# A two-block transformer kernel in split fp32: the opening's orders in the filter and the mixer changed, and the forgetting attention with tiles halved around its logits, named PSUM banks and values products behind the tiles

## The reference

```python
def hybrid_mixer(h, w_in, b_forget, conv_w, conv_b, conv_ln_g, conv_ln_b, w_out):
    z = h @ w_in                      # a 512, g 512, q 512, k 512, v 512, f 8 columns
    ...
    u = a * jax.nn.sigmoid(g)
    u = causal_depthwise_conv(u, conv_w, conv_b)             # width 31
    u = jax.nn.silu(layer_norm(u, conv_ln_g, conv_ln_b))
    log_f = jax.nn.log_sigmoid((f_logit + b_forget).astype(jnp.float32))
    att = forgetting_attention(q.reshape(shp), k.reshape(shp), v.reshape(shp), log_f)
    ...
    return jnp.concatenate([u, att], axis=-1) @ w_out

def forgetting_attention(q, k, v, log_f):      # 8 heads of 64, blocks of 128 rows, causal
    ...
        logits = logits + cum[:, :, q0:kl, None] - cum[:, :, None, :kl]
        p = jax.nn.softmax(jnp.where(mask, logits, NEG_INF), axis=-1)

x = x + rms_norm(hybrid_mixer(rms_norm(x, g), ...), g2)
x = x + rms_norm(memory_cross_attention(rms_norm(x, g), rms_norm(mem, g), ...), g2)
x = x + rms_norm(squared_relu_mlp(rms_norm(x, g), w_up, w_down), g2)
# second block: MLA layer and Hyena layer (FFT convolutions with learned filters), each with a conv FFN
```

## Time and profile before

| | us |
|---|---|
| runs | 2100.52, 2098.52, 2098.56, median 2098.56 |
| profiled execution | 2100.5 |
| its span | 2098.7 |
| PE busy | 2011.9 (96%) |
| PE weight load busy | 1672.6 (80%) |
| DVE busy | 1272.0 (61%) |
| POOL busy | 983.0 (47%) |
| ACT busy | 861.7 (41%) |

### The profile page before, as it was taken

The page is one execution under the profiler, slowest core; times in us unless marked ns, Lnnn a source line. Parts: engine busy times, 40 slices in busy tenths (PEclk is TensorE's granted clock), DMA queues, the critical chain, the costliest instruction groups (busy, mean ns, idle before and its releaser), DMA issues.

```text
span 2098.7 us, 23678 instructions
## 1 busy us (share of the span) xinstructions
PE 2011.9 (96%) x9667; PEld 1672.6 (80%) x9667; DVE 1272.0 (61%) x1568; ACT 861.7 (41%) x1254; POOL 983.0 (47%) x476
## 2 busy tenths in 40 slices
PE   6999989999999999999999999999998999999997
PEld 4777778778888887787888888878887888888886
DVE  7677845462245435663677775545679657778644
ACT  5746775631122234774443333232322244333322
POOL 5579454454444433123444444444667654444443
PEclk9999999999999999999999999999999999999999
DMA  6432123112222230121222222215222312222221
GB/s 206 154 123 81 41 81 106 65 71 101 101 99 86 97 113 27 43 71 47 71 86 98 101 101 100 84 63 185 101 71 101 121 61 101 100 101 92 89 101 40
DMA packets 35041, 193.00 MB, mean 92 GB/s; under 512 B 4400, under 2 KB 4992, under 8 KB 15413
## 3 DMA queue, kind: packets, MB, share of 16 engines
q1 hardware_dynamic: 34932, 191.49, 26.1%
HBM read 177.77 MB, written 13.64 MB: 91 GB/s over the span
## 4 chain that ended last, share of the span: by engine, by line
PE 77%; DVE 11%; ACT 6%; POOL 4%; issue 2%; DMA 0%; SPq 0%; ACTq 0%; DVEq 0%; POOLq 0%
PE ps L159 73%; PE ps L158 3%; DVE TMP L182 2%; POOL WL L182 1%; POOL CO L182 1%; DVE X L182 1%; DVE X L194 1%; DVE YL L182 1%; PE ps L167 1%; DVE ps L194 1%; POOL YF L182 1%; DVE ps L182 1%; ACT WH L175 1%; ACT PP L176 0%; DVE VG L182 0%
## 5 line engine op out<-in xcount | busy, mean ns | idle before, releaser
L182 POOL TENSOR_TENSOR WL<-W,WH 128x2048 fp32r<-128x2048 f32 (+3 forms) x165 | 650.5, 3948 | 860.5 <-ACT WH L175 857.0
L159 PE MATMUL ps<-HH,WL 128*128 128x512 f32 (+1 forms) x1408 | 545.6, 388 | 15.4 <-DVE HL L194 7.9
L159 PE MATMUL ps<-HH,WH 128*128 128x512 f32 (+1 forms) x1408 | 538.8, 383 | 0.0
L159 PE MATMUL ps<-HL,WH 128*128 128x512 f32 (+1 forms) x1408 | 538.8, 383 | 0.0
L175 ACT ACTIVATE WH<-W 128x2048 fp32r<-128x2048 f32 (+2 forms) x145 | 269.4, 1858 | 316.8 <-PE ps L159 316.8
L159 PEld LDWEIGHTS ps<-HH,WL 128*128 128x128 f32 x1408 | 265.3, 188 | 74.9 <-DVE HL L194 9.9
L159 PEld LDWEIGHTS ps<-HH,WH 128*128 128x128 f32 x1408 | 265.2, 188 | 51.9
L159 PEld LDWEIGHTS ps<-HL,WH 128*128 128x128 f32 x1408 | 265.6, 189 | 50.7 <-issue 0.2
L182 DVE TENSOR_TENSOR MRL<-MID,MRH 128x512 fp32r<-128x512 f32 x76 | 177.4, 2365 | 162.3 <-ACT MRH L175 162.3
L159 PE MATMUL ps<-MRH,WL 128*128 128x512 f32 x608 | 238.2, 392 | 3.3 <-ACT PAD L175 2.2
L159 PE MATMUL ps<-MRH,WH 128*128 128x512 f32 x608 | 236.7, 389 | 0.0
(11 more groups left out here) (370 smaller groups left out, 3284.3 us busy)
## 6 DMA issues: line engine op xcount, KB each, us to landing
W<-in_up SPq DMA_DIRECT2D x44, 1024.0 KB, 4.8
W<-in_down SPq DMA_DIRECT2D x22, 1024.0 KB, 4.8
W<-in_w_up SPq DMA_DIRECT2D x16, 1024.0 KB, 4.8
W<-in_w_down SPq DMA_DIRECT2D x16, 1024.0 KB, 4.8
W<-in_hy_in SPq DMA_DIRECT2D x12, 1024.0 KB, 4.8
kd<-STG SPq DMA_DIRECT2D x36, 256.0 KB, 2.0
KB<-kd SPq DMA_DIRECT2D x8, 1024.0 KB, 5.8
W<-in_win_ag SPq DMA_DIRECT2D x4, 1024.0 KB, 4.8
```

The source lines that it names most:

```text
L159: return self.eng.matmul(out, lhs, rhs, start=start, stop=stop)
L182: return QUIET if self.eng is None else self.eng.tensor_tensor(out, a, b, op)
```

## The change

The chunks of q and k: the first one (tiles 0 and 1) is put ahead of v's two, so chunk 6 is qk, 7 and 8 are v, 9 to 11 the others. In the filter PE waits for the first half of chunk 0's low part alone, copies of WP are done earlier on ACT and POOL, and ACT's copies of x for the first norm (`x_high`) are parted from the squares (`x_square`). In the mixer's start, the column sums and transposes of the norm and the forget gate are done between the tiles of "ag". Tiles of q and k from 3 on are cut into two halves, one before the logits of the next head and one behind; banks are named (`on(i)` sets the turn), three (`here`) for this head's transposes and values, and three (`there`) for the next head's logits. The convolution's steps on DVE are 6 at head 0 and 14 at head 1 in place of 7 a head; the memory norm's scaling and the centring of the convolution come at heads 3 and 4; the squares of the centred values are made by POOL; the first chunk of w_out takes its k tiles in the order 4, 5, 6, 0, 1, 2, 3, 7. The DMA of the constants `tri` is issued ahead of chunk 6.

```diff
 
 CHUNKS = [
-    ("dft_cs", 0, 2048), ("dft_kx", 0, 256), *[("win_ag", i, 2048) for i in range(4)], *[("win_v", i, 2048) for i in range(2)],
-    *[("win_qk", i, 2048) for i in range(4)], *[("w_mk", i, 2048) for i in range(2)],
+    ("dft_cs", 0, 2048), ("dft_kx", 0, 256), *[("win_ag", i, 2048) for i in range(4)], ("win_qk", 0, 2048),
+    *[("win_v", i, 2048) for i in range(2)], *[("win_qk", i, 2048) for i in range(1, 4)], *[("w_mk", i, 2048) for i in range(2)],
...
-
-                wh, wl = chunk(n)
+                if (n, part) == (0, 0):
+                    pe.wait_ge(*at("w_high", n))
+                    pe.wait_ge(*at("w_low", n, "first"))
+                    wh, wl = place(n)
+                else:
...
 
             def turn_f(n):
 
                 if n == 0:
+                    column_sum([(("xcol",), DG, ("xacc", 7), None, ("xcol",))])
+                if n == 2:
+                    spread("rs", 0, slot=4)
+                if n == 4:
                     ps = open_bank("ft_")
                     pe.wait_ge(*at("fs_"))
                     for b in range(4):
                         ins = pe.turn(ps[:, 8 * b:8 * b + 8], FZ[:, blk(b)], IDT[0:8, 0:8])
...
+                turn[0] = i
+
+            def qk_steps(n, first, last):
+                wh, wl = chunk(CH["win_qk"][n // 2])
+                ps = bank("qk", n) if first else open_bank("qk", n)
+                for k in range(first, last + 1):
+                    col = (2 * k + n % 2) * 128
+                    ins = pe.mm3(ps[:], wh[:, col:col + 128], wl[:, col:col + 128], *feat(k), k == 0, k == 7)
+                if last == 7:
+                    ins.then_inc(*up(acc, ("qk", n), *[("w_used", CH["win_qk"][n // 2])] * (n % 2)))
+
+            qk_steps(0, 0, 7)
+            qk_steps(1, 0, 7)
             vb = [open_bank("v", b) for b in range(4)]
...
-                for i in range(4):
+
+                def mask(i):
+                    if i != 1:
+                        on(places[max(i - 1, 0)])
+                        open_bank("fs", h, max(i, 1))
                     nk = 128 * (i + 1)
                     pe.mm(logits(h, i)[:, nk - 128:nk], IDR[:], MKR[:], i != 1, False, True)
+
+                for i in range(3):
+                    mask(i)
...
                 for i in range(4):
+                    if i == 3:
+                        mask(3)
                     nk = 128 * (i + 1)
...
+                for k in (4, 5, 6, 0, 1, 2, 3, 7):
+                    pe.wait_ge(*at("cat", k))
...
+            fox_s(0, (g0, g1, v1))
+            on(v2)
+            qk_steps(2, 0, 7)
+            here, there = [g0, g1, v1], [v0, v2, v3]
             for h in range(8):
-                fox_t(h)
+                fox_t(h, here)
+                if h < 5:
+                    on(there[2])
+                    qk_steps(h + 3, 0, 3)
+                if h == 5:
+                    mem_k(0, (0, 1), 0, 3, (c0, c1))
                 if h < 7:
-                    fox_s(h + 1)
+                    fox_s(h + 1, (there[0], there[1], here[0]))
+                if h < 5:
+                    qk_steps(h + 3, 4, 7)
+                if h == 5:
+                    mem_k(0, (0, 1), 4, 7)
+                if h == 6:
+                    on(there[2])
+                    column_sum([(("cq2",), CO2[:, j, :], ("csq", j), None, ("cq2",) if j == 3 else None)
+                                for j in range(4)])
+                    mem_k(1, (0,), 0, 7, (here[2],))
                 if h == 7:
-                    mem_k(1, 1)
-                qk_tile(h + 4)
-                fox_pv(h)
+                    mem_k(1, (1,), 0, 7, (c0,))
+                    on(c1)
+                    spread("crs", slot=20)
...
                     spread("mr", slot=28, nb=2)
-                if h == 4:
-                    total("cmu", ap=DG[:], need=("cacc", 3))
...
-                if h == 5:
-                    mem_k(0, 0, 1)
-                if h == 6:
...
+                    on(c0)
+                    total("cmu", ap=DG[:], need=("cacc", 3))
+                here, there = [there[0], there[1], here[0]], [there[2], here[1], here[2]]
...
-                act.wait_ge(*at("h", 1, 1, 3, 1))
+                act.wait_ge(*at("wpt", 1, 1, 1))
                 act.act(HH[:, k, :], X[:, k, :], ACT.Identity, par("g_mix_pre", k)).then_inc(*out(("hn", 0, k, "hi")))
+
...
+                        if m == 3 and o == 0 and c == 0:
                             wp_high(0, 1, 0)
                             wp_high(0, 1, 1)
+                        if m % 2 and o == 1:
+                            x_high(4 * c + m - 1)
+                            x_high(4 * c + m)
                 for c in range(2):
...
+            qk_high(0)
+            products(9, 12)
+            qk_high(1)
+            weights(8)
+            products(13, 16)
+            weights(9)
+            for b in range(4):
+                act.wait_ge(*at("v", b))
...
                     dst = QKB[e, j % 2][0:64, 1, :] if m else QKA[e, j % 2][64 - 64 * e:128 - 64 * e, 0, :]
                     low(dst, bank("qk", n)[hd, :], QKA[e, j % 2][hd, m, :], ("k" if m else "q", j, e),
                         *[("free", "qk", n)] * e)
-                if n < 2:
-                    convolve(4, 3)
+
+            convolve(2, 3)
+            qk_out(0)
+            convolve(6, 3)
+            qk_out(1)
+            convolve(20, 3)
...
                     low(PTL[:, q], bank("ft", h, j)[:, 0:q.stop - q.start], PTH[:, q], ("pt", h, j), ("free", "ft", h, j))
+                if h == 6:
+                    mem_k_low(0, 1)
                 if h < 7:
                     fox_max(h + 1)
-                    convolve(3, 3)
-                    if h in (4, 5):
-                        scaled_memory(4 * h - 16, 4 * h - 15)
+                    if h == 1:
+                        convolve(3, 3)
+                    if h in (3, 4):
+                        scaled_memory(4 * h - 12, 4 * h - 9)
                     fox_rcp(h + 1)
-                    if h in (4, 5):
-                        scaled_memory(4 * h - 14, 4 * h - 13)
-                convolve(4, 3)
+                if h == 0:
+                    convolve(6, 3)
+                if h == 1:
+                    convolve(200, 3)
+                if h in (3, 4):
+                    centred(2 * h - 6, 2 * h - 5)
                 if h == 7:
-                    for j in range(4):
-                        low(HL[:, j, :], CO[:, j, :], HH[:, j, :], ("cat", j))
-                qk_out(h + 4)
-                fox_low(h)
...
-            h_low(4, 7)
+            h_low(4, 5)
             wp_low(0, 1, 0)
...
+            taps(11, 16)
             weights(9)
-            taps(15, 24)
+            taps(17, 19)
             weights(10)
+            taps(20, 24)
             twins(2)
...
-            weights(6)
             sp.wait_ge(*at("rs", 0))
             load("tri", DG[:], t["consts"][:, 256:768])
+            weights(6)
```

233 lines of the change are left out of this document (121 added, 112 removed).

## The result

The change takes 2107.15 us (median of 5 runs, 2104.97 to 2109.34) against 2100.11 us (2098.52 to 2100.76) for the kernel before: a ratio of 1.0039 with a 95% interval of 1.0027 to 1.005. It is slower by 0.39%; 2096 in a range of 2084 to 2107 was predicted, and a gain was the likelier sign.

What follows compares the result with a forecast made beforehand. PE, busy 96% of the span, bounds the kernel, so only waits and low clock can be won. PE's count and clock gave -5.9, chunk 15 took back 1.9, one fall 1.6: -2.2, so 2096 us, range 2084 to 2107.

Steps and rivals of the forecast that it cites:

- 1.2 for the first w_out chunk: Heads 3 to w_out: 1.2 us of PE wait at that chunk, within 3.0 us of small waits.
- -2.2: Predicted shift at the second w_out chunk, counting one clock fall of 1.6 us, before the third head's logits.
- t(0): First transposes: a wait of 2.2 us in place of 3.32, ending at 197.0, 2.6 us ahead in PE's count.
- MRS: Tile 4's first half waits for ACT to free its bank, behind six convolution steps: about +3.3 us.
- fox_s(3): Head 3's logits wait for tile 4's bank, freed by DVE behind eleven convolution steps: about +4.6, taken as 5.0 us.
- three falls, +1.0: Case where each of three new waits costs a 1.6 us clock fall, making the shift +1.0 us.
- The filter's term: Opening: the 1.85 us WP wait and the low clock after it go, about -3.6 us.
- now stand inside it: Start: column sums and spreads (1.6 us) move from ahead of the gate GEMM into it; net so far -4.0 us.
- A: Rival, chance 0.26: waits at heads 0 to 2 are shorter; 2090.6 us, down to 2084.
- C: Rival, chance 0.12: the filter edit does nothing, so 3.6 us of gain is gone; 2100 us, up to 2103.
- B: Rival, chance 0.20: DVE, ACT and PE loop at heads 0 to 2, head 3's logits wait 8 us; 2104, up to 2108.
- D: Rival within the forecast's 0.42: POOL's additions slowed beside DVE's convolutions, chunk 8 ready 2.6 us later; 2099 us.

Runs made afterwards that it cites:

- free banks: The change with the first w_out tiles opened in two other banks that are free early, nothing else; 2100.69 us, ratio 1.001.
- early copy: As free banks, and ACT copies the second w_out chunk ahead of the four silu steps; 2100.93 us, ratio 1.001.
- the filter alone: The kernel before with only the filter's part of the change; 2093.15 us, ratio 0.9978.
- filter and start: The kernel before with the change's filter part, mixer start and earlier constants DMA, v and heads as before; 2097.37 us, ratio 0.999.
- convolution behind tiles: As free banks, with DVE's convolution steps of heads 0 and 1 placed behind qk_out and fox_low; 2100.68 us, ratio 1.0006.
- chunk 8 early: As early copy, with ACT's copy of v's second half ahead of products 9 to 12 and POOL's low part behind tap 8; 2097.76 us.
- convolution spread: As chunk 8 early, with DVE's convolution steps spread over heads 0 to 2 and all centring at head 4; 2096.81 us, ratio 0.9987.
- the filter undone: The change with its filter edits taken out, all else kept, w_out banks too; 2108.69 us, ratio 1.006.

## Why the prediction was wrong

**The step that failed** is "1.2 for the first w_out chunk" among the small waits. It measured 6.07, and 6 us at clock 0.53 followed, 2.8 us more. I had followed the data of that chunk (the cat tiles, its low part) and took the banks for free; the tenant of `there[1]` is head 7's values. With other banks alone 5.44 us of the +7.55 go, which is shown; 1.93 us for chunk 15 come in that wait's place. Without that the change is +2.1 at the landmark and 2100.69 us.

**The rest, from -2.2 to +2.1, stands ahead of w_out, and most of it is clock.** With the free banks PE is ready for chunk 15 at 306.1 us (308.06 less the wait of 1.93), where the sum has 301.7 (300.1 and one fall). The wait itself came out as forecast, 1.93 for 1.9; chunk 15 is late by as much as PE, behind silu, CATH and a table load in ACT's queue, and the early copy shows that this place is worth 1.1 us. The 4.4 us are: 2.6 at the end of t(0) (199.6 in place of 197.0), which come from the gates (below); 1.7 for a fall behind MRS, at 213, that I had not counted; 0.9 since the low clock behind fox_s(3) took 2.5 and not 1.6; less 1.3 of waits that were shorter. About 0.5 stays open. Of the forecast's cases the one with three falls, +1.0, was the nearest, though t(0) had none.

**What held.** WP's wait went, its copies now at 41.14. Gates at 97.24 (97.2 predicted), with a wait of 1.99. Chunk 5 took the constants' wait back: 1.52 (2.0 predicted). Chunk 8: 3.65 (3.7), though PE and the chunk both came 2.4 us later than in the sum. MRS: 3.34 (3.3). fox_s(3), 4.21 (4.6 to 5.0), by the low parts of QKA behind the eleven steps. Heads 3 to 7: 0.7 + 1.27 (1.8). t(0): 0.73 (2.2), the one that was well off; PE came there later.

**The filter and the start.** The filter's term held: at its last matmuls PE is 3.8 us ahead in the change and 3.9 with the filter alone, where I had 3.6. What was wrong in the opening is my reading of the start, "now stand inside it" at no loss. At 120 us the change is 1.5 us ahead where I had 4.0. Of these 2.5 us, 1.7 is the fall behind the wait at 97.24 (it did not come in three of the seven profiles with this wait), and the rest is time of PE for the sums.

**Rivals.** A (short waits at heads 1 and 2) and C (no filter gain) did not happen. B has the right sign, but its mechanism, the loop of DVE, ACT and PE, did not: fox_s(3) waited 4.2 us and not 8. D: chunk 8's low part was ready at 175.8 us, 2.3 later than the 173.5 of the sum, but D is not the reason: POOL's squares started at 151.41 and not at 149.2, with the gates late, and six of its additions took 8.16 us, 1.36 each as before.

## What to carry to other kernels

A reordering is bounded by the banks as much as by the data: when the order of k is changed so that the late tile comes last, list the last tenant of every bank that the first matmul opens. Work that is moved away may have stood in the shade of a copy or a low part; ask first what PE would do there instead. Look at the instruction that frees or copies for the next chunk, and how deep it stands in ACT's and DVE's queues: the w_out banks were worth 5.4 us here, the place of chunk 8's copy about 3. And before a shift between two profiles is put down to an edit, compare the granted clock behind each wait that both have: here the same wait fell in one and not in the other, at 1.6 to 3 us a time, as much as several of the edits.

## What the runs showed of the hardware

The length of a wait alone did not decide on the clock. A wait of 1.99 us at 127.75 in the kernel before was followed by full clock (1.00 in the earlier trace rows, and in the next window below); the wait of 1.99 us for WL in the change by 0.68. That wait, at the same place behind the same instructions, stands in seven profiles: the clock fell in four (the change, free banks, early copy, filter and start) and held in three (convolution behind tiles, chunk 8 early, convolution spread).

The same holds where the whole program is the same. In the kernel before, that next window, and in the second block two waits and the windows around them:

```profile
129.90:152.10 22.20, 22.20 (x98) 17.93 (x97) 17.95 (x26) 11.81 (x13) 19.29 (x13) 1.00 0.16 52
...
1596.78 0.63 PE L167 MATMUL ps<-IDT,TMP 128*128 128x128 f32 x4 [2.32 <-DVE ZL L182]
...
1648.53 0.79 PE L159 MATMUL ps<-HYH,WL 128*128 128x512 f32 x1 [2.00 <-POOL HYL L182]
...
1596.00:1602.00 6.00, 5.22 (x21) 4.26 (x21) 4.16 (x9) 0.60 (x1) 4.71 (x6) 0.72 0.84 339
1648.00:1653.00 5.00, 4.47 (x13) 3.58 (x14) 4.86 (x9) 1.41 (x5) 5.00 (x7) 0.66 1.01 419
```

The same two waits in the changed kernel, and the windows 7.5 us later:

```profile
1604.42 0.63 PE L167 MATMUL ps<-IDT,TMP 128*128 128x128 f32 x4 [2.31 <-DVE ZL L182]
...
1654.59 0.50 PE L159 MATMUL ps<-HYH,WL 128*128 128x512 f32 x1 [2.02 <-POOL HYL L182]
...
1603.50:1609.50 6.00, 5.08 (x27) 4.27 (x28) 5.67 (x11) 1.20 (x2) 5.77 (x7) 1.00 0.84 341
1655.50:1660.50 5.00, 5.00 (x24) 4.10 (x23) 4.86 (x9) 1.46 (x4) 5.00 (x7) 1.00 1.01 423
```

0.72 and 0.66 against 1.00 and 1.00. The Trainium skill (TensorE: Matmul & The Clock Gate, "What's actually happening") says that the gate's window runs on its own and doesn't restart with the kernel. I infer from it that the same gap may or may not cost a fall; these rows are in line with that and don't test it.

The price can be read from the profiles of all fourteen kernels here, since behind the landmark they run the same program. Apart from a fall right at the landmark, which changes nothing in these times, and the low stretch at the very end, which all have, they differ in three places. From the landmark to the end it takes 1665.2 to 1665.4 us in the four profiles without a fall on the way, 1666.4 to 1666.7 in four with one near 1400 us, 1668.5 in two with the two above (the kernel before is one), and 1669.6 to 1669.7 in three with all three; one with the first and the last of them has 1668.2. So the spans of the change and of the kernel before differ by 3.1 us beyond the landmark with no edit there. Runs of one kernel lie 4 us apart, with the steps spread and with the filter undone up to 7; such falls are the likely reason, but that was not traced run by run.
